# Two gate transfers of 2 MB become one of 4 MB in the late experts of a decoder layer

## The reference, cut to what matters

```
y = (silu(x @ w_gate[e]) * (x @ w_up[e])) @ w_down[e]     # w_gate, w_up: 2048 x 512, w_down: 512 x 2048
```

## Time and profile before

| | us |
|---|---|
| median of three runs (1470.96 to 1471.92) | 1471.56 |
| the profiled execution | 1471.65 |
| its span, first to last instruction | 1469.9 |
| outside the span | 1.75 |
| TensorE busy | 1348.9 (92%) |
| VectorE busy | 475.6 (32%) |
| ScalarE busy | 255.2 (17%) |
| DMA, mean over the span | 359 GB/s |

### The profile page before, as it was taken

How to read it: one execution, slowest core, us unless ns; L and a number is a source line. 1 busy time by engine, 2 the same in 40 slices (tenths; PEclk the granted TensorE clock), 3 DMA queues, 4 the chain that set the end, 5 groups by cost and what they waited for, 6 DMA issues and landing times.

```text
span 1469.9 us, 25136 instructions
## 1 busy us (share of the span) xinstructions
PE 1348.9 (92%) x10754; PEld 822.0 (56%) x10755; DVE 475.6 (32%) x1200; ACT 255.2 (17%) x602; POOL 53.0 (4%) x85
## 2 busy tenths in 40 slices
PE   9999999999999899798788788887888899999996
PEld 7899999998898344343333333333333444444442
DVE  2667665677676213011111101010101022222225
ACT  2202221323212231111110111001111111111114
POOL 1000000200050000000000000000000000000003
PEclk9999999999999999999989989898898799999998
DMA  9666443589796999999999999999999999999992
GB/s 348 217 185 253 144 143 131 190 315 344 286 386 258 429 426 426 429 422 417 428 428 429 428 430 429 428 428 428 428 428 428 425 424 410 426 426 428 428 426 82
DMA packets 66509, 527.86 MB, mean 359 GB/s; under 512 B 6223, under 2 KB 28887, under 8 KB 31207
## 3 DMA queue, kind: packets, MB, share of 16 engines
q1 hardware_dynamic: 64320, 524.41, 87.1%
q10 hardware_dynamic: 2104, 2.21, 0.4%
HBM read 512.33 MB, written 14.26 MB: 358 GB/s over the span
## 4 chain that ended last, share of the span: by engine, by line
PE 35%; DMA 34%; DVE 2%; issue 1%; POOL 1%; ACT 1%; DVEq 0%; ACTq 0%; POOLq 0%
DMA raw<-in_w_up 28%; PE ps L2252 7%; PE ps L2567 7%; PE ps L2623 6%; PE ps L2578 3%; DMA raw<-in_w_down_cuts 3%; PE ps L291 3%; DMA more<-in_w_down 3%; PE ps L1453 1%; PE ps L1584 1%; PE ps L2225 1%; PE ps L2265 1%; PE ps L2619 1%; PE ps L2276 1%; PE ps L1529 1%
## 5 line engine op out<-in xcount | busy, mean ns | idle before, releaser
L2252 PE MATMUL ps<-raw,xT 128*32 128x512 f32 x1488 | 202.8, 678 | 87.1 <-DMA raw<-in_w_up 58.9
L1468 DVE TENSOR_TENSOR xT<-ps,ffn_gain 128x512 f32<-128x512 f32 x33 | 22.8, 691 | 488.4 <-PE ps L2225 488.4
L2252 PEld LDWEIGHTS ps<-raw,xT 128*32 128x32 f32 x1488 | 43.6, 116 | 211.8 <-DMA raw<-in_w_up 86.2
L182 PE MATMUL ps<-mixT_hT,raw 128*128 128x264 f32 x608 | 137.9, 387 | 0.4 <-DVE more L602 0.4
L291 PE MATMUL ps<-mixT_hT,raw 128*128 128x132 f32 x960 | 127.8, 279 | 2.6 <-PEq L1047 1.7
L182 PEld LDWEIGHTS ps<-mixT_hT,raw 128*128 128x128 f32 x608 | 114.6, 190 | 21.1 <-DVE mixT_hT L598 0.9
L2623 PE MATMUL ps<-more,space 128*128 128x512 f32 x256 | 123.4, 611 | 0.0
L291 PEld LDWEIGHTS ps<-mixT_hT,raw 128*128 128x128 f32 x960 | 116.1, 190 | 8.0 <-issue 6.2
L1453 PE MATMUL ps<-x_res,mine 128*32 128x512 f32 (+1 forms) x792 | 106.6, 656 | 0.3 <-DVE mine L1927 0.3
L2265 PEld LDWEIGHTS ps<-fold,mixT_hT 128*128 128x128 f32 x512 | 68.6, 208 | 47.6 <-issue 37.2
L2805 DVE TENSOR_TENSOR x_res<-ps,x_res 128x512 f32<-128x512 f32 x51 | 35.3, 691 | 158.3 <-PE ps L2623 151.1
(11 more groups left out here) (447 smaller groups left out, 1354.2 us busy)
## 6 DMA issues: line engine op xcount, KB each, us to landing
raw<-in_w_gate SPq DMA_DIRECT2D x60, 2048.0 KB, 16.4
raw<-in_w_down_cuts SPq DMA_DIRECT2D x40, 2048.0 KB, 15.1
more<-in_w_up SPq DMA_DIRECT2D x32, 2048.0 KB, 15.4
raw<-in_w_up SPq DMA_DIRECT2D x31, 2048.0 KB, 16.6
raw<-in_mix_chunks SPq DMA_DIRECT2D x59, 1024.0 KB, 6.1
more<-in_w_down_cuts SPq DMA_DIRECT2D x15, 2048.0 KB, 15.8
more<-in_w_down SPq DMA_DIRECT2D x8, 2048.0 KB, 16.7
more<-in_w_gate_cuts SPq DMA_DIRECT2D x8, 2048.0 KB, 16.9
```

What stands on the lines that cost most here:

```text
L182: return nc.tensor.matmul(ps[:, j, 0:NT], core.raw[:, q % NCH, k * GW + j * P:k * GW + (j + 1) * P], xT[:, core.groups[g].k0 + c * CK + k, ...
L1468: core.nc.vector.tensor_tensor(rt["xT"].rearrange("p k (i s) -> p k i s", i=EI), core.ps[:, 2, :].rearrange("p (k i s) -> p k i s", k=EK, ...
L2252: last = nc.tensor.matmul(ps[own, (GATE, UP)[m], :], xT[:, k, i * SLOTS:(i + 1) * SLOTS], weights, start=(i == 0 and k < 4), stop=(i == EI ...
```

## The change

For experts 5 to 31 the two gate items are issued as one transfer of 4 MB (`load_whole`). Its source is both halves of w_gate[e]; its destination is places 0 and 1, which lie side by side. It waits until both gate items of the expert before are used (`chunk_used` at `used + EI`, EI = 2), and it raises the landing semaphore of place 0 alone. The up items are issued as before, each after its own predecessor is used. On TensorE, the wait for the landing of place 1 is left out for these experts (`elif not (whole and at == 1)`); expert 4 keeps its two waits. The two lines in `all_landed` belong to a branch for more than 32 rows in an expert.

```diff
+def whole_gate(core, w, e):
+    rows = w["w_gate"][0].rearrange("e (i p k) c -> e i p (k c)", i=EI, p=P)
+    src = rows[bass.ds(e, 1), :, :, :].rearrange("o i p c -> (o p) i c")
+    return src, core.raw[:, 0:2 * EI, :].rearrange("p (i a) c -> p i (a c)", i=EI)
...
+            def load_whole(e, used):
+                sp.wait_ge(q["chunk_used"], used + EI)
+                src, dst = whole_gate(core, w, e)
+                sp.dma_start(dst, src).then_inc(landed[0], 16)
+                for at in range(EI, 2 * EI):
                     sp.wait_ge(q["chunk_used"], used + (at + 1))
                     item(e, at)
...
                 with sp.Fori(FULL + 1, NE) as e:
-                    load_late(e, e * (2 * EI) + ((FULL + 1) * ECH - (FULL + 1) * 2 * EI))
+                    load_whole(e, e * (2 * EI) + ((FULL + 1) * ECH - (FULL + 1) * 2 * EI))
...
             def all_landed():
                 sp.wait_ge(q["first_steps"], 32)
+                sp.wait_ge(landed[0], 16 * (NE - 1))
+                sp.sem_inc(landed[1], 16 * (LATE - 1))
...
-            def project(m, i, n):
+            def project(m, i, n, whole=False):
...
-                else:
+                elif not (whole and at == 1):
                     pe.wait_ge(landed[at], n * 16 + (0 if at <= EXTRA and not (isinstance(n, int) and n == 0) else 16))
...
                 for q4 in range(4):
                     e = i * 4 + q4
+                    whole = not (ple and q4 == 0)
                     pe.wait_ge(q["x_copied"], e + 1)
-                    project(0, 0, e)
-                    project(0, 1, e)
+                    project(0, 0, e, whole)
+                    project(0, 1, e, whole)
```

More of the change, by code:

```diff
@@ L2019, in load_late @@
                     item(e, at)
+            def load_whole(e, used):
[3 more added lines that the diff above has]
+                for at in range(EI, 2 * EI):
+                    sp.wait_ge(q["chunk_used"], used + (at + 1))
+                    item(e, at)
             def first():
```

## The result

The changed kernel takes 1490.46 us (median of 5 runs, 1483.62 to 1494.29) against 1471.56 (5 runs, 1470.96 to 1472.92): ratio 1.0113, 95% interval 1.0095 to 1.0130. It is 1.1% slower. The forecast of no change was wrong, and so was its range; the time went where the rival "the lead is too short" put it (1485 us). The profiled execution took 1492.86 us, with a span of 1491.1 against 1469.9: 21.2 us longer.

What follows compares the result with a forecast made beforehand. The DMA queue was taken as the bound from 480 to 1417 us, with TensorE close behind. Terms: 1471.65 + 0 + 0.2 - 0.5 = 1471.3 us, no change; range 1468.6 to 1477.

Steps and rivals of the forecast that it cites:

- the lead is too short: Rival, experts 9 to 31: pair's need exceeds the lead, mean 0.6 us lost per expert, 14 us, 1485 us; chance 0.11.
- One issue less per expert, worth 0: Experts 5 to 31: 27 pairs replace 54 items; issue and fixed transfer costs are hidden in the full queue, 0 us.
- TensorE starts gate 0 later, hidden: Each merged expert: gate 0 starts at the pair's landing T, gates take 5.3 us; delay lies inside 3.6 us idle time.
- The issue waits for both gates: Experts 9 to 31: pair issued at T + 5.4, leaving 4.4 us until the queue runs empty; 0 us lost.
- the need: Lead a transfer needs to avoid loss: between 2.2 and 3.8 us, taken as 2.5; far bound for a pair 4.4.
- the estimate of 54 us: Merged gate loads: 27 transfers less at about 2.0 us fixed each would save 54 us if nothing hid them; 0 taken.
- Experts 5 to 8: Experts with extra embedding work on TensorE: leads 4.3, 4.3, 5.2, then 3.2 for pair 9; cost taken as 0.2 us.
- The hand-over: From expert 31 to finish: TensorE starts finish some 2.5 us sooner; gain between 0 and 1.6 us, taken as 0.5.
- The lower rate: Rival: pairs reading alternately from two halves 2 MB apart move slower, up to 34 us, 1506 us; chance 0.05.
- falling transfer costs: Rival: each of 27 merges saves 0.15 us or more, 1467 us, or 1466 to 1468 without finish dips; chance 0.06.
- TensorE as the bound: Rival: TensorE needs 4.0 us more per expert, above 3.6 us slack, costing 9 us, 1480 us; chance 0.02.
- The sign named for it: Short-lead sign: slices below 425 GB/s in 700 to 1120 us, with issue to landing of pairs under 13 us.

Runs made afterwards that it cites:

- experiment 2: Kernel before, all loads as they were, but TensorE waits for gate 1's landing before starting gate 0 (experts 5 to 31): 1471.86 us, ratio 0.9995.
- experiment 4: Changed kernel plus 20 unused matmuls at the end of each expert from 8 on, keeping TensorE warm: 1474.96 us, ratio 1.0019 against the kernel before.
- experiment 3: Changed kernel with pairs in two alternating sets of places, issued half an expert period earlier; first finish pieces loaded after expert 31: 1472.10 us, ratio 1.0001 against before.
- experiment 7: Changed kernel, but the pair is issued only when all four items of the expert before are used, so the queue is empty: 1646.04 us.
- experiment 5: Changed kernel with two 2 MB transfers replacing the pair, TensorE waiting for both before gate 0: 1486.68 us, ratio 1.0090 against the kernel before.

## Why the prediction was wrong, step by step

*What bounds the kernel* was right: TensorE's waits moved by tens of microseconds in experiments 2 and 4 with no loss of their own, and the time followed the queue's rate in every kernel.

*One issue less per expert, worth 0*: right. Experiment 3 has the merged transfers with nothing else to disturb them, and it equals before within 0.13%.

*TensorE starts gate 0 later, hidden*: right (experiment 2). Its waits for gates were foreseen at 70 us and measured 83.0, those for up items gone. The gates took until T + 5.76, not T + 5.4.

*The issue waits for both gates*: the step that failed. The lead was well found, 4.4 foreseen and 4.0 measured on average (3.4 to 4.85). The failure is the need: "between 2.2 and 3.8 ... I take 2.5", 0 us lost. It is between 4.35 and 4.87, about the far bound of 4.4 or above it, and the loss is 0.77 us an expert (21 experts whose pair is issued between 690 and 1125 us) where the lead is 4.0. Both ends of the range were read from landings, and a landing shows the slowest of 16 engines alone. The lower end, 2.2, is right for an empty queue (2.9 for a pair) but says nothing of engines that run dry 2 to 3 us before the landing. The upper end, was misread. There the landing came 4.9 to 5.0 us behind the one ahead and I wrote "no loss that can be read". The kernel before around that issue at 674.86, by single microseconds:

```profile
675.00:676.00 1.00, 1.00 (x16) 0.29 (x11) 0.00 (x0) 0.00 (x0) 0.00 (x0) 1.00 0.88 311
676.00:677.00 1.00, 1.00 (x12) 0.27 (x8) 0.00 (x0) 0.57 (x1) 0.00 (x0) 1.00 0.96 328
```

The dip is there, 311 to 328 GB/s with 3.8 us of lead; only the slowest engine, which sets the landing, happened to be spared. At a lead of 3.5 to 4 an issue lost anything from 0.0 to 1.7 us, so one without loss proves nothing. A landing can mislead the other way too. In the same trace gate 1 of expert 7 landed 6.0 us behind gate 0, whose lead had been 4.8 us. But gate 0 had landed in time, at 643.27, and an instruction packet held one engine from 644.80 for 1.07 us; the lead had no part in it that can be read.

The Trainium skill, "DMA: Bandwidth & Descriptors", section "Anatomy of one DMA", measured its 2.0 us fixed for each DMA on transfers that GpSimd issues; SyncE issues these, and into an empty queue they cost 2.9 us (experiment 7). So the estimate of 54 us in the prediction stood on a figure of another path. The Trainium skill's advice to coalesce, in its section "Rules for kernel authors", is for many small transfers; for these of 2 MB it brought nothing in a full queue (experiment 3).

*Experts 5 to 8*: lead of pair 9 foreseen at 3.2, measured 2.6; 0.2 us foreseen, and by landings 3.4 lost less 1.6 that before loses there too, 1.8. The same need was mis-sized, but the instruction packets fall in this stretch in both kernels, so how much of the 1.8 is the lead's stays open.

*The hand-over*: -0.5 foreseen; the last stage gave back 1.1 us, and the dip of the earlier trace rows is gone: no slice of 7.5 us between 1150 and 1450 us is below 417 GB/s. In the dip before, transfers were issued with leads of 3.8 to 5.8 us, after the change with 8 us or more in that part. Inside its bounds (0 to 1.6).

*The rivals.* The short lead came true, with 0.6 us an expert in its sum against 0.8 measured, 1485 us against 1490.5; its need of 4.4 was about right, its mean loss a little small, and its chance of 0.11 rested on the earlier trace rows. The lower rate (experiment 3, and experiment 5 from the other side), falling transfer costs and TensorE as the bound did not show. *The sign named for it* was half right: slices below 425 GB/s, yes, but issue to landing of pairs was 14.7 us in the middle, not under 13. With a lead of 4.0, 9.8 of data and a loss of 0.8 that is what it must be; under 13 belongs to a queue already empty (experiment 7).

What stays open: why the 16 engines drift some 3 us apart, why the first packet of an engine that stood idle takes up to 2.3 us, and whether the form of the pair adds something at a short lead. The runs change when a transfer is issued, not how the engines share it.

## What to carry to other kernels

Where the DMA queue is the bound, merging loads into the places just used moves the issue to the last of them, and what that costs is set by the lead that is left: find it for every issue and keep it above 5 us here, not above the fixed cost of one transfer. Don't judge a lead by when the next transfer landed, since a landing shows the slowest engine only; look at GB/s in windows of one microsecond around the issue, at many issues, and at what other queues put on the same engines meanwhile. If a merge is wanted anyway, it needs places of its own (experiment 3), and even then it brings nothing in a queue that is full.

## What the runs showed of the hardware

- A transfer issued while the item ahead still had 4.0 us to its landing let 9 of 16 DMA engines run dry at once (the issue at 1004.79), with 180 GB/s in the worst microsecond. After 755 us no issue with a lead of 4.87 us or more lost over 0.02 us (54 issues).
- An issue into an empty queue costs 2.9 us (12.7 to landing for 9.8 of data) for one transfer of 4 MB, and about the same for two of 2 MB (12.6 to 13.0). The first packet starts 1.0 us after the issue.
- A packet of the instruction queue, 16 KB, holds one DMA engine for about 1.0 us, and one landing of 2 MB then came up to 1.5 us late in a full queue (737.9 us after the change).
- A 4 MB transfer that reads 16 KB rows from two halves 2 MB apart keeps the full rate, 9.79 us; with rows of 8 KB from both halves, 2 MB took 4.95 to 4.98 us instead of 4.89.
- TensorE's clock reached the DMA time: added matmuls, 97.0 us of them between 720 and 1120 us, raised the granted clock from 0.83 to 1.00, and the kernel was 15.5 us faster for it, since the used places came free sooner.
